# A hybrid decoder step on one core: the merged stage of recurrence and cache gather in a new order

## The reference

```python
# GLA on the prompt: 4 heads of 64, S_t = diag(a_t) S_{t-1} + k_t^T v_t, o_t = q_t S_t
scores = jnp.einsum('bhtd,bhsd,bhtsd->bhts', qc, kc, jnp.exp(rel))
o = (jnp.einsum('bhts,bhse->bhte', scores, vc)
     + jnp.einsum('bhtd,bhde->bhte', qc * jnp.exp(bcum), s))
s_new = (jnp.exp(b_end[:, :, 0, :, None]) * s
         + jnp.einsum('bhsd,bhse->bhde', kc * jnp.exp(b_end - bcum), vc))
...
# NSA of the samples: compression MLP over blocks of 32 cached rows at stride 16
hid = (jnp.einsum('bnrhd,rde->bnhe', r[:, :-1] + pe[...], w1[:CMP_STRIDE])
       + jnp.einsum('bnrhd,rde->bnhe', r[:, 1:] + pe[...], w1[CMP_STRIDE:]) + b1)
...
# and the scores of all cached selection keys
s_sc = jnp.einsum('bthgd,bhtnsd->bhgtns', qf, k_sel)
```

## Time and profile before

| what | value |
|---|---|
| median of 3 runs | 2028.47 us (2026.05 to 2029.22) |
| the profiled execution, its own time | 2025.64 us |
| its span, first to last instruction | 2023.4 us |
| busy TensorE / VectorE / ScalarE / GpSimd | 89% / 53% / 31% / 11% of the span |
| mean granted TensorE clock | 0.931 of full speed |

### The profile page before, as it was taken

One profiled execution on the slowest core, in us unless ns is written; L12 is line 12 of the kernel. 1 busy time (PEld: TensorE's weight loads), 2 busy tenths in 40 slices (PEclk: granted clock), 3 DMA queues, 4 the chain that ended last, 5 costly groups with the idle time before them and its releaser, 6 DMA issues. The chain is left out here.

```text
span 2023.4 us, 32058 instructions
## 1 busy us (share of the span) xinstructions
PE 1804.9 (89%) x12811; PEld 1671.2 (83%) x12811; DVE 1076.4 (53%) x1875; ACT 635.3 (31%) x1140; POOL 213.8 (11%) x257
## 2 busy tenths in 40 slices
PE   6989999778899959898795489999999999999997
PEld 6989989766677747777672279999999999999997
DVE  5462672256677735555456666644555444444544
ACT  6523321155555533233233335412111111212111
POOL 1000000023333231222212110000000000000000
PEclk9989999878999978899766689999999999999999
DMA  7621144320000044545364555111111112111102
GB/s 193 88 97 32 53 132 140 101 56 12 14 11 1 1 157 152 183 175 196 111 138 98 193 155 180 63 42 42 41 41 41 41 44 81 42 41 41 41 22 84
DMA packets 172272, 170.85 MB, mean 84 GB/s; under 512 B 49788, under 2 KB 156884, under 8 KB 168452
## 3 DMA queue, kind: packets, MB, share of 16 engines
q1 hardware_dynamic: 168692, 131.54, 22.3%
q0 software_dynamic: 2304, 33.56, 4.3%
q10 hardware_dynamic: 1168, 4.26, 0.8%
HBM read 136.98 MB, written 36.56 MB: 86 GB/s over the span
## 5 line engine op out<-in xcount | busy, mean ns | idle before, releaser
L58 PE MATMUL pm<-hidH,weights 128*128 128x344 f32 x768 | 247.2, 322 | 4.4 <-DVE weights L3252 4.4
L58 PE MATMUL pm<-hH,wuH 128*128 128x344 f32 x768 | 246.4, 321 | 3.1 <-DVE wuL L3247 3.1
L59 PE MATMUL pm<-hidL,weights 128*128 128x344 f32 x768 | 246.1, 320 | 0.0
L60 PE MATMUL pm<-hidH,weights 128*128 128x344 f32 x768 | 245.8, 320 | 0.0
L60 PE MATMUL pm<-hH,wuL 128*128 128x344 f32 x768 | 245.0, 319 | 0.0
L59 PE MATMUL pm<-hL,wuH 128*128 128x344 f32 x768 | 245.0, 319 | 0.0
L58 PE MATMUL pz<-hH,winH 128*128 128x344 f32 x600 | 201.6, 336 | 10.7 <-DVE zb L830 6.5
L59 PE MATMUL pz<-hL,winH 128*128 128x344 f32 x600 | 195.0, 325 | 0.0
L60 PE MATMUL pz<-hH,winL 128*128 128x344 f32 x600 | 194.9, 325 | 0.0
L3256 DVE SCALAR_TENSOR_TENSOR act<-pm,onat 128x344 f32<-128x344 f32 x96 | 49.3, 515 | 244.3 <-PE pm L60 244.2
L3267 DVE TENSOR_TENSOR onat<-pm,onat 128x344 f32<-128x344 f32 x256 | 129.0, 513 | 70.3 <-PE pm L60 70.3
(11 more groups left out here) (602 smaller groups left out, 3575.3 us busy)
## 6 DMA issues: line engine op xcount, KB each, us to landing
uact<-in_w_up_dram SPq DMA_DIRECT2D x16, 1024.0 KB, 6.8
hs<-in_w_down_dram SPq DMA_DIRECT2D x16, 1024.0 KB, 4.9
raw<-in_w_in_dram SPq DMA_DIRECT2D x24, 512.0 KB, 3.8
vS_scratch<-page_rows SPq DMA_DIRECT2D x16, 512.0 KB, 4.2
hold<-vS_scratch SPq DMA_DIRECT2D x8, 1024.0 KB, 11.6
wo<-in_w_out_dram SPq DMA_DIRECT2D x12, 512.0 KB
act<-in_w_out_dram SPq DMA_DIRECT2D x12, 512.0 KB, 4.0
onat<-qkT_scratch SPq DMA_DIRECT2D x18, 256.0 KB, 4.3
```

Of the source, the lines that this page charges most:

```text
L58: nc.tensor.matmul(out, wH, mH, start=(k == 0), stop=False)
L59: nc.tensor.matmul(out, wH, mL, start=False, stop=False)
L60: last = nc.tensor.matmul(out, wL, mH, start=False, stop=(k == n - 1))
```

## The change

In every half the score tokens come first (`ORDER`), then the raw keys and the compression values. Their sums move from the `HID` bank to the bank of `og`, and a copy of their own (`copy_scores`, slot 9 on ACT) takes them out; `hid_ready` is waited for at `use(it, 2)` instead of `use(it, 0)`. On DVE `queries` move from slot 4 to slot 2, ahead of `update`, and `differences` are split over slots 5, 6 and 7, each behind the slot's `merge`. `copy_fill` of slot 3 goes from DVE to ACT. `turn_keys` and its copy move one slot later (5 to 6, 6 to 7), `keys_by_values` from slot 8 to 9. POOL issues both gathers of the next sample ahead of the next `keys`, and at the start `keys(0)` ahead of the masks. SP loads `w1` in halves, the first ahead of everything but the first chunk. The gates' addition, the sigmoid and a load of the table for exponentials come at the very start. The last chunk's levels start at slot 4 (`first_level`), so the ninth iteration is gone.

```diff
@@ -1629,7 +1629,7 @@
-        carry = sb("carry", [1, 1])
+        carry, warm = sb("carry", [1, 1]), sb("warm_exp", [1, 1])
@@ -1639,22 +1639,26 @@
-        SCP = HIDP[0][:, 2 * P:3 * P]
+        ORDER = (2, 2, 0, 0, 1, 1)
+        SCP = og[:, 2 * P:3 * P]
...
-        by_act = (0, 2, 4, 5, 6, 7, 8, 10)
-        by_dve = (1, 3, 9, 11)
+        by_act = (0, 2, 3, 4, 5, 6, 7, 8, 10)
+        by_dve = (1, 9, 11)
+
+        first_level = lambda c: 6 if c < NCH - 1 else 4
...
         def copies(s, n):
...
-        zeroed, gated, setup, masked = sem("zeroed"), sem("gated"), sem("setup"), sem("masked")
+        zeroed, gated, q_laid, setup, masked = sem("zeroed"), sem("gated"), sem("q_laid"), sem("setup"), sem("masked")
...
-            [sem(f"z_in{i}") for i in range(2)], sem("w_in"), [sem(f"gathered{i}") for i in range(2)],
+            [sem(f"z_in{i}") for i in range(2)], [sem(f"w_in{i}") for i in range(2)], [sem(f"gathered{i}") for i in range(2)],
...
+        sc_kept = sem("sc_kept")
@@ -1668,10 +1672,17 @@
+                def load_w1(half):
+                    at = slice(half * 8, half * 8 + 8)
+                    for j in range(2):
+                        sp.dma_start(w1[:, j, at, :, :],
+                                     io["w1S"].rearrange("p (j r w e) -> p j r w e", j=2, r=16, w=2)[:, j, at, :, :]).then_inc(w_in[half], 16)
+
                 load_z(0)
+                load_w1(0)
                 load_z(1)
...
-                sp.dma_start(w1[:, :, :, :, :].rearrange("p j r w e -> p (j r w e)"), io["w1S"][:, :]).then_inc(w_in, 16)
+                load_w1(1)
@@ -1709,6 +1720,7 @@
+                keys(0)
@@ -1742,11 +1754,10 @@
-                keys(0)
                 for c in range(NCH - 1):
                     gather(c + 1, 0)
+                    gather(c + 1, 1)
                     keys(c + 1)
-                    gather(c + 1, 1)
...
             def _(pe):
@@ -1758,39 +1769,41 @@
-                        token = kv[half][:, (f % 2) * 4 + u, f // 2, :, :].rearrange("p h d -> p (h d)")
+                        token = kv[half][:, (f % 2) * 4 + u, ORDER[f], :, :].rearrange("p h d -> p (h d)")
...
                 def use(s, n):
...
-                    if f < 4:
-                        j = f // 2
-                        if n == 0:
-                            pe.wait_ge(w_in, 16)
-                            if s:
-                                pe.wait_ge(hid_ready, s)
+                    j = ORDER[f]
+                    if j < 2:
+                        if n in (2, 8):
+                            pe.wait_ge(w_in[half], 32)
+                        if n == 2 and s:
+                            pe.wait_ge(hid_ready, s)
...
-                                                        start=(j == 0 and r == 0), stop=(h == 1 and j == 1 and r == 15))
+                                                        start=(j == 0 and r == 0), stop=(j == 1 and r == 15))
...
-                        if n == 4:
-                            pe.wait_ge(gated, 1)
+                        if n == 0:
+                            pe.wait_ge(q_laid, 1)
+                            if s:
+                                pe.wait_ge(sc_kept, s)
+                        if n == 6 and s:
+                            pe.wait_ge(og_copied, s)
...
-                            r = half * 8 + (f - 4) * 4 + u
+                            r = half * 8 + (f % 2) * 4 + u
...
-                                                    start=False, stop=r == 15)
+                                                    start=True, stop=True)
...
                 def level(c, l):
...
-                        if c == 0:
-                            pe.wait_ge(setup, 1)
@@ -1820,6 +1833,8 @@
                 def outputs(c):
...
+                    if c == NCH - 1:
+                        pe.wait_ge(sc_kept, NS)
@@ -1830,29 +1845,31 @@
-                for it in range(NCH + 1):
-                    for n in range(NFILL if it < NCH else 4):
-                        if it < NCH:
-                            fill(it, n)
+                for it in range(NCH):
+                    for n in range(NFILL):
+                        fill(it, n)
...
-                        if n >= 6 and it < NCH:
-                            level(it, n - 6)
-                        if n and it < NCH:
+                        if first_level(it) <= n < first_level(it) + 8:
+                            level(it, n - first_level(it))
+                        if n:
...
-                        elif n == 0 and it:
+                        elif it:
...
-                        if n == 5:
+                        if n == 6:
                             turn_keys(it)
-                        if n == 8:
+                        if n == 9:
                             keys_by_values(it)
+                use(NCH - 1, NFILL - 1)
+                outputs(NCH - 1)
...
             def _(act):
...
+                nc.scalar.activation(warm[:, :], keep["eps"][0:1, :], ACT.Exp)
...
                 def copy_fill(s, n):
@@ -1864,8 +1881,12 @@
                 def copy_hidden(s):
...
-                        nc.scalar.activation(hid[h * 64:h * 64 + 64, :, s, :], HID[h][0:64, :, :], ACT.Copy)
-                    nc.scalar.activation(sTa[:, :, s * 8:s * 8 + 8], SCP.rearrange("p (r c) -> p r c", r=16), ACT.Copy).then_inc(hid_copied, 1)
+                        last = nc.scalar.activation(hid[h * 64:h * 64 + 64, :, s, :], HID[h][0:64, :, :], ACT.Copy)
+                    last.then_inc(hid_copied, 1)
+
+                def copy_scores(s):
+                    act.wait_ge(f_used, NFILL * s + 8)
+                    nc.scalar.activation(sTa[:, :, s * 8:s * 8 + 8], SCP.rearrange("p (r c) -> p r c", r=16), ACT.Copy).then_inc(sc_kept, 1)
...
                 def sizes(c):
@@ -1886,13 +1907,15 @@
-                        if n == 6:
+                        if n == 7:
...
+                        if n == 9:
+                            copy_scores(it)
...
             def _(dve):
@@ -1959,34 +1982,36 @@
+                nc.vector.tensor_tensor(gates[:, :], gates[:, :], gbias[:, :], ALU.add).then_inc(gated, 1)
...
-                    nc.vector.tensor_copy(qbd[rws, :, h * 4:h * 4 + 4], q2[rws, :, :].rearrange("p g s -> p s g"))
+                    last = nc.vector.tensor_copy(qbd[rws, :, h * 4:h * 4 + 4], q2[rws, :, :].rearrange("p g s -> p s g"))
...
-                nc.vector.tensor_tensor(gates[:, :], gates[:, :], gbias[:, :], ALU.add).then_inc(gated, 1)
-                for it in range(NCH + 1):
-                    for n in range(NFILL if it < NCH else 5):
-                        if n in by_dve and it < NCH:
+                last.then_inc(q_laid, 1)
+                for it in range(NCH):
+                    for n in range(NFILL):
+                        if n in by_dve:
                             copy_fill(it, n)
...
                             add_hidden(it - 1)
...
-                        if n == 4:
-                            if it:
-                                update(it - 1)
-                            if it < NCH:
-                                nc.vector.drain()
-                                queries(it)
-                        if n == 5 and it + 1 < NCH:
-                            differences(it + 1, range(0, 4))
-                        if n == 6 and it + 1 < NCH:
-                            differences(it + 1, range(4, 9)).then_inc(diffs, 1)
-                        if n >= 6:
-                            merge(it, n - 6)
+                        if n == 2:
+                            nc.vector.drain()
+                            queries(it)
+                        if n == 4 and it:
+                            update(it - 1)
+                        if first_level(it) <= n < first_level(it) + 8:
+                            merge(it, n - first_level(it))
+                        if it + 1 < NCH and n in (5, 6, 7):
+                            last = differences(it + 1, (range(0, 4), range(4, 6), range(6, 9))[n - 5])
+                            if n == 7:
+                                last.then_inc(diffs, 1)
+                add_hidden(NCH - 1)
+                update(NCH - 1)
```

## The result

The changed kernel takes 1979.12 us (median of 4 runs, 1976.65 to 1982.8), the one before 2027.26 (4 runs, 2021.55 to 2029.22): ratio 0.9767, 95% interval 0.9753 to 0.9782. The forecast was 1978, range 1971 to 1995. The profiled execution took 1982.8 us, span 1980.4.

What follows compares the result with a forecast made beforehand. TensorE sets the pace, busy 27.3 of 30.7 us an iteration, so its waits and half clock can be won. Savings of 37.5 (iterations), 7.5 (start) and 5.4 (end) sum to 50.4 us: 1978 us, 80% range 1971 to 1995.

Steps and rivals of the forecast that it cites:

- The steady iteration: Loop iteration priced by slots at full speed: 25.5 us against 30.75, from three waits, the half clock and 0.15 unplaced.
- The waits: TensorE's three waits in each iteration, for hid_ready, queries and the merge before level 1, all go: 3.4 us an iteration.
- the wait of level 1: TensorE's 1.68 us wait for merge 0, put down to nine differences ahead of it on DVE; expected to go.
- The half clock: Clock at 0.50 right behind the 1.12 us wait, costing 1.6 us an iteration; expected to become 1.00 without waits.
- Rival 2: Clock still falls once an iteration, at score tokens and transposes in slots 1 and 2: 13 us, 1991; chance 0.13.
- The rule of the Trainium skill: Warns only of much longer idle gaps; by it the half clock need not go: 11 us stay, sum 1989.
- Seven iterations and the last two levels: Loop total: 6 x 25.5 + 26.5, plus 1.0 unplaced, is 180.5 against 218.0 us; 37.5 saved.
- The start: Up to the end of iteration 0: w1 wait goes, less gather delay and cold clock; 7.5 us saved, bounds 3 and 10.
- The end: Short ninth iteration of 9.4 us becomes 4.0 of last use, outputs, update and hand-overs; 5.4 us saved.
- Rival 3: A transfer or the keys arrive late, or the merge chain still holds levels: up to 11 or 12 us; chance 0.15.
- rival 4: Slower: keys behind gather(it, 1) and a late store delay the queries, so level 0 stalls; 2037 us; chance 0.03.
- The total: Sum of loop, start and end savings: 50.4 us, giving a forecast of 1978 us.

## Why the prediction was right

- **The steady iteration** (forecast 25.5): 25.4 in every iteration at 1.00, in five profiles of the changed loop. Slot prices read at full speed add up, and no queue came short.
- **The waits** went as forecast, but for the wait of level 1 the reason was too narrow. The forecast gave it to the split. The runs show that the split alone removes it, that sooner queries alone remove it too, together with the wait of level 0, and that the split then adds nothing.
- **The half clock** was the wrong step: "the trace has the drop behind the wait in every iteration", and "TensorE has no wait left in the loop, so I expect 1.00". Queries alone kept the wait in all iterations and lost the half clock in four; the changed kernel had no wait and met it three times, 1.6 us each (27.0 against 25.4). The trace of the kernel before spoke against "the drop behind the wait in every iteration", outside the iterations that the prediction read. In iteration 2 the clock falls ahead of the wait:

```profile
809.80:810.20 0.40, 0.40 (x6) 0.40 (x5) 0.39 (x1) 0.00 (x0) 0.40 (x1) 1.00 0.00 0
810.60:811.00 0.40, 0.40 (x3) 0.17 (x1) 0.00 (x0) 0.39 (x2) 0.40 (x1) 0.50 0.00 0
...
812.94 2.08 PE L1778 MATMUL pr<-hs,w_heads 64*128 64x128 f32 x16 [0.61 <-DVE onat L1959]
```

  Its seven iterations also hold eleven such stretches, not seven: three in iteration 1, two each in iterations 2 and 7 (the clocks 0.84, 0.89 and 0.89). Of the eleven, three were left in the first profile of the changed kernel and none in the second. So a gain from the clock came, but not for the reason given, and its size is partly luck. Rival 2 may have named the right kind of place, but it was slots 7 and 8 instead of 1 and 2, and not once an iteration. The rule of the Trainium skill that the prediction weighed ("TensorE: Matmul & The Clock Gate", section "Why this matters for your kernels") is borne out in one half: a gap of 1.1 us does not bring the clock down by itself. But idle gaps, which are all that the section names, are not the whole of it: the stretch ahead of 837.3 shows 3.40 us busy of 3.40, and the clock falls.
- **Seven iterations and the last two levels** (forecast 37.5 saved): from 767.9 to the end of slot 11 near 951.4 it is 183.5 against 218.0, so 34.5. The three half-clock stretches (4.8) are more than the 3.0 that are missing.
- **The start** (forecast 7.5): 45.4 - 38.2 = 7.2. Two errors cancel, which is luck. The gather was hardly delayed (first fill 741.33, before 741.08), which is 1.25 better than the 1.5 taken. TensorE stayed at half clock from 741.3 to about 752, now with work in all of these 10.7 us; in the kernel before 5.9 us of work fell into half clock. Half of the difference, some 2 us, is an estimate of what was lost; 0.5 was charged.
- **The end** (forecast 5.4): 9.4 less the 3.8 from 951.4 to 955.2, so 5.6. The size is right and the reading behind it was not. The forecast had "levels 6 and 7, each waiting for a merge". In the kernel before neither waits (they start at 993.72 and 995.35); it is `outputs` that waits 2.4 us for the merge of level 7, which stands behind `add_hidden` on DVE, a sixth wait that the earlier trace rows lacks:

```profile
998.43 1.97 PE L1827 MATMUL pr<-hold,pTg 128*128 128x64 f32 x8 [2.37 <-DVE pTg L1935]
```

  The ninth iteration put back costs 2.8 us, with a wait of 2.0 for that merge, so the gain is not all from it. Part of the rest is the clock: these products took 1.97 us here at half clock, and 1.10 in the other two profiles.
- **Rival 3**, margins of a transfer: half 0 was never late. For half 1 the margin hangs on the order on GpSimd, which the forecast brings up only in rival 4, for the queries and not for this transfer. Taken back, it costs about 5 us.
- **The total** (50.4 saved): 47.3 in the stage, 48.1 by the medians. The untouched rest varies by up to 7 us from one execution to the next.

## What to carry to other kernels

Where engines run in written order, moving one long instruction on a helper engine to an earlier place can remove two waits at once: move that first, profile again, and only then split the rest. Add up an iteration by slots at full speed and compare it with the measured one; the difference is the list of waits, plus the clock. A clock that falls beside a wait need not fall because of it: look for an iteration in which it falls ahead of the wait (iteration 2 here), or remove the wait alone, before charging the one to the other.

## What was not expected of the hardware

A small copy on VectorE stood still beside a large product on GpSimd. While `keys(0)` ran from 737.22 to 741.72, a copy of 64 x 32 elements took 4.46 us and ended with the product. It took 0.92 us in the kernel before, where only short instructions ran beside it on GpSimd, and the same copy of the other head took 0.18 us in both:

```profile
737.22 4.50 POOL L1712 TENSOR_TENSOR hold<-zq,hold 128x2048 f32<-128x2048 f32 x1 [0.24 <-ACT hold L1897]
737.30 4.46 DVE L1990 COPY qbd_n<-q 64x32 f32<-64x32 f32 x1
...
741.79 1.04 DVE L1991 COPY q<-q 64x32 f32<-64x32 f32 x1
```

In the loop of the changed kernel the merges and copies out of PSUM that run beside `keys` keep their length (0.72 and 0.69 us). The Trainium skill ("GPSIMD Engine Reference", section "Specifications") says that GpSimd shares its SBUF interfaces with VectorE, and that the two contend when VectorE's instruction is in a two-port mode or has two inputs in SBUF. This copy has one input, and no view here shows its mode, so the row fits the section but does not settle which case it is. `q_laid` came with the end of that copy at 741.8, 1.3 us ahead of the first score tokens at 743.1.
